# Merge with ten logit buffers, two output-weight buffers and an earlier split of the branch weights

## The chip, the core and the metric

The kernel runs on one core of one Trainium2 chip. Its engines work side by side, each through its own instructions in order: TensorE (PE) multiplies matrices, VectorE (DVE), ScalarE (ACT) and GpSimd (POOL) work on elements, and SyncE (SP) issues the transfers between the chip's main memory (HBM) and the core's memory (SBUF). The engines meet only at semaphores. TensorE writes its sums into PSUM, which has eight banks of 512 columns. The metric is the time of one launch in microseconds of the device, as the median of several runs.

## What is computed

Two layers of a network on 1024 latent rows and 256 context rows, each 1024 wide. Each layer normalises its rows, runs four branches (two kinds of attention, a gating MLP and a delta rule), and then merges them. The change is in the merge of each layer and in the memory around it:

```python
def merge(h, branches, pgate):
    silu_gates = jnp.split(jax.nn.silu(pgate), N_BRANCH, -1)
    acc = None
    for i in range(N_BRANCH):
        term = jax.nn.sigmoid(h @ w_gate[l, i]) * ((branches[i] * silu_gates[i]) @ w_branch[l, i])
        acc = term if acc is None else acc + term
    return acc @ w_out[l]

out_x = merge(hx, (ya_x, yb_x, yc_x, yd_x), px_g)
x_new = layer_norm(DEEPNORM_ALPHA * x + gt_x * out_x) * ln_g[l] + ln_b[l]
```

The last layer needs no context rows, so it merges 1024 rows where the first merges 1280.

## The kernel before

`build` runs the phases of a layer one after the other, with a barrier of all engines between them: `modulation`, `normalise_rows`, the four branches, `merge`, `output`. `normalise_rows` leaves the normalised rows, turned and split into a high and a low part, in `m.hh` and `m.hl` (40 KB of each partition for each). The class `Dense` spreads the products `h @ w_gate`, which are the logits of the merge gates, over the branches as filling work for TensorE and stores them in HBM as `gate_sums`. These products are all done when `apply_gates`, the first part of `merge`, ends. So the rows are no longer read in what follows.

The rest of `merge` is the place of the change. It goes through `products`, a list of triples (f, b, n): f is one of 8 blocks of 128 output columns, b one of 4 branches, n one of the chunks of rows (256, 512 and 512 rows in the first layer, two of 512 in the last). A block has 12 products in the first layer and 8 in the last, which makes 96 and 64 products, numbered u. For each product:

- SP loads the logits from `gate_sums` (line 2171) into one of `LOGITS = 4` buffers of 512 columns, once product u - 4 has been multiplied.
- ACT takes their sigmoid in place (line 2200).
- TensorE makes the branch product (lines 89 to 91: three matmuls for each of two row blocks of the weights, since an fp32 product is made of high and low parts), into bank u % 8.
- DVE multiplies the two (line 2241). For b = 0 the result goes to the block's accumulator `acc` (memory of `m.dv`), else to one of two term buffers (`TERMS = 2`, memory of `out_ds` and `raw_ds`), each of which must have been added before it is written again.
- POOL adds the term to the accumulator (line 2262).

Three more things run through the same queues. The weights of the four branches for a block (512 KB) are loaded by SP into one buffer `w` (line 2162) and split by `cut`: ACT writes the high part (line 2194), DVE the low part (line 2225), and TensorE begins a block only when its low part is there (`w_low`). The finished accumulator of block f - 1 is stored by SP at product b = 2, n = 0 of block f, after a wait for all its additions (line 2180). The weights of `output` are brought in 16 pieces of 256 KB, two for each block (`out_piece`: where u % EVERY is 3), through one buffer `wo` (line 2177), and split into the memory of `m.hh` and `m.hl` by ACT (line 2204) and DVE (line 2246). The order of all this is the order in which the loops are written. Before the change ACT splits the next block's weights after branch 2, and DVE after the first product of branch 3:

```python
if b == 2 and n == n_c - 1 and f + 1 < KD:    # scalar
    cut(f + 1)
if b == 3 and n == 0 and f + 1 < KD:          # vector
    cut(f + 1)
```

Of the kernel before, what the change touches and what calls it, by code (L numbers as in the profile page):

```python
# [5 lines left out]
F32 = mybir.dt.float32  # L6
F32R = mybir.dt.float32r
ALU = mybir.AluOpType
ACT = mybir.ActivationFunctionType
# [2106 lines left out]
                fill.cut(pool)  # L2116


def merge(nc, m, l):


    chunks = m.dense.chunks
# [2 lines left out]
    with ExitStack() as st:  # L2125
# [4 lines left out]
        halves = lambda x: x[:].rearrange("p (s a) b c -> p s (a b) c", s=2).rearrange("p s (b k) c -> p s b k c", k=2)  # L2130
        w = sb("w", [P, 4, 2, P])
        wh, wl = halves(m.dense.wh), halves(m.dense.wl)
        LOGITS, TERMS = 4, 2
        logit = sb("logit", [P, LOGITS, 512])
        term = [m.dense.out[:], m.dense.raw[:].rearrange("p k c -> p (k c)")]
        acc = m.dv[:].rearrange("p t c -> p (t c)").rearrange("p (s c) -> p s c", s=2)
        names = [f"logit_in{s}" for s in range(LOGITS)]
        wo = sb("wo", [P, 512])
        with phase(nc, "w_in", "w_high", "w_low", "sigm", "branched", "multiplied", "added", "stored0", "stored1",
                   "wo_in", "wo_high", "wo_low", *names) as (  # L2140
                block, w_in, w_high, w_low, sigm, branched, multiplied, added, stored0, stored1, wo_in, wo_high, wo_low,
                *logit_in):
            stored = [stored0, stored1]
            products = [(f, b, n) for f in range(KD) for b in range(4) for n in range(n_c)]
            EVERY = 2 * n_c

            def out_piece(u):

                i = u // EVERY
                return (i, i // 2, slice(i % 2 * 512, i % 2 * 512 + 512)) if u % EVERY == 3 else None  # L2150

            def nth(f, b, n):
                return (3 * f + b - 1) * n_c + n

            @block.sync
            def _(sp):
                sp.wait_ge(m.dense.stored, 16 * m.dense.units * n_c)

                def weights(f):
                    if f >= 1:  # L2160
                        sp.wait_ge(w_low, f)
                    sp.dma_start(w[:], m.d_wmerge[l, 4 * f:4 * f + 4, :, KD:KD + 2].rearrange("b p k c -> p b k c")
                                 ).then_inc(w_in, 16)

                weights(0)
                weights(1)
                for u, (f, b, n) in enumerate(products):
                    at, width = chunks[n]
                    if u >= LOGITS:
                        sp.wait_ge(multiplied, u - LOGITS + 1)  # L2170
                    sp.dma_start(logit[:, u % LOGITS, 0:width], m.d_raw[:, 8 + 4 * f + b, at:at + width]
                                 ).then_inc(logit_in[u % LOGITS], 16)
                    if out_piece(u):
                        i, k, part = out_piece(u)
                        if i:
                            sp.wait_ge(wo_low, i)
                        sp.dma_start(wo[:], m.d_wout[l, k, :, part]).then_inc(wo_in, 16)
                    if b == 2 and n == 0 and f >= 1:
                        sp.wait_ge(added, 3 * n_c * f)
                        sp.dma_start(m.d_acc[:, f - 1, lo:], acc[:, (f - 1) % 2, lo:]).then_inc(stored[(f - 1) % 2], 16)  # L2180
                        if f + 1 < KD:
                            weights(f + 1)
                sp.wait_ge(added, 3 * n_c * KD)
                sp.dma_start(m.d_acc[:, KD - 1, lo:], acc[:, (KD - 1) % 2, lo:]).then_inc(stored[(KD - 1) % 2], 16)
                for s in range(2):
                    sp.wait_ge(stored[s], 16 * KD // 2)

            @block.scalar
            def _(act):
                def cut(f):  # L2190
                    act.wait_ge(w_in, 16 * (f + 1))
                    if f >= 2:
                        act.wait_ge(branched, (f - 1) * 4 * n_c)
                    act.activation(wh[:, f % 2], w[:], ACT.Copy).then_inc(w_high, 1)

                cut(0)
                for u, (f, b, n) in enumerate(products):
                    act.wait_ge(logit_in[u % LOGITS], 16 * (u // LOGITS + 1))
                    own = logit[:, u % LOGITS, 0:chunks[n][1]]
                    act.activation(own, own, ACT.Sigmoid).then_inc(sigm, 1)  # L2200
                    if out_piece(u):
                        i, k, part = out_piece(u)
                        act.wait_ge(wo_in, 16 * (i + 1))
                        act.activation(m.hh[:, k, part], wo[:], ACT.Copy).then_inc(wo_high, 1)
                    if b == 2 and n == n_c - 1 and f + 1 < KD:
                        cut(f + 1)

            @block.tensor
            def _(pe):
                for u, (f, b, n) in enumerate(products):  # L2210
                    at, width = chunks[n]
                    if b == 0 and n == 0:
                        pe.wait_ge(w_low, f + 1)
                    if u >= 8:
                        pe.wait_ge(multiplied, u - 7)
                    for k in range(2):
                        mm = split_products(pe, m.ps[:, u % 8, 0:width], wh[:, f % 2, b, k], wl[:, f % 2, b, k],
                                            yh[:, 2 * b + k, at:at + width], yl[:, 2 * b + k, at:at + width], k == 0, k == 1)
                    mm.then_inc(branched, 1)

            @block.vector
            def _(dve):
                def cut(f):
                    dve.wait_ge(w_high, f + 1)
                    dve.tensor_tensor(wl[:, f % 2], w[:], wh[:, f % 2].bitcast(F32), ALU.subtract).then_inc(w_low, 1)  # L2225

                cut(0)
                for u, (f, b, n) in enumerate(products):
                    at, width = chunks[n]
                    dve.wait_ge(sigm, u + 1)  # L2230
                    dve.wait_ge(branched, u + 1)
                    if b == 0:
                        dst = acc[:, f % 2, at:at + width]
                        if f >= 2:
                            dve.wait_ge(stored[f % 2], 16 * (f // 2))
                    else:
                        at_term = nth(f, b, n)
                        dst = term[at_term % TERMS][:, 0:width]
                        if at_term >= TERMS:
                            dve.wait_ge(added, at_term - TERMS + 1)  # L2240
                    dve.tensor_tensor(dst, logit[:, u % LOGITS, 0:width], m.ps[:, u % 8, 0:width], ALU.mult
                                      ).then_inc(multiplied, 1)
                    if out_piece(u):
                        i, k, part = out_piece(u)
                        dve.wait_ge(wo_high, i + 1)
                        dve.tensor_tensor(m.hl[:, k, part], wo[:], m.hh[:, k, part].bitcast(F32), ALU.subtract
                                          ).then_inc(wo_low, 1)
                    if b == 3 and n == 0 and f + 1 < KD:
                        cut(f + 1)

            @block.gpsimd
            def _(pool):
                for u, (f, b, n) in enumerate(products):
                    at, width = chunks[n]
                    if b == 0:
                        continue
                    pool.wait_ge(multiplied, u + 1)
                    at_term = nth(f, b, n)
                    if b >= 2:
                        pool.wait_ge(added, at_term - n_c + 1)  # L2260
                    own = acc[:, f % 2, at:at + width]
                    pool.tensor_tensor(own, own, term[at_term % TERMS][:, 0:width], ALU.add).then_inc(added, 1)


def output(nc, m, l, out):

    tiles = range(0 if l < DEPTH - 1 else CT, NT)
    src = m.d_x if l == 0 else m.d_x1
    wo_h, wo_l = m.hh[:, :, 0:D], m.hl[:, :, 0:D]
    AHEAD = 4  # L2270
    with ExitStack() as st:
        sb = lambda n, s, d=F32: st.enter_context(nc.sbuf_tensor(f"{n}_ou{l}", s, d))
# [119 lines left out]
def build(nc, d_x, d_c, d_const, d_rope, d_vec, d_bvec, d_wmod, d_win, d_winr, d_ws, d_bs, d_wuq, d_wukv,  # L2392
# [12 lines left out]
    with ExitStack() as st:  # L2405
# [8 lines left out]
        m.gate_c = sb("gate_c", [P, 16])  # L2414
        m.dv = sb("dv", [P, NT, BR])
        m.ab = sb("ab", [P, NT, 16])
        m.hh = sb("hh", [P, KD, ROWS], F32R)
        m.hl = sb("hl", [P, KD, ROWS], F32R)
        with phase(nc, "loaded") as (block, loaded):
            @block.sync  # L2420
            def _(sp):
# [6 lines left out]
                dve.memset(m.eps[:], EPS)  # L2428
        for l in range(DEPTH):
            modulation(nc, m, l)  # L2430
            with ExitStack() as layer:
                m.dense = Dense(nc, m, l, layer)
                normalise_rows(nc, m, l)
                gating_mlp(nc, m, l)
                latent_attention(nc, m, l)
                differential_attention(nc, m, l)
                delta_net(nc, m, l)
                merge(nc, m, l)
                m.dense.free()
            output(nc, m, l, out)  # L2440
        return m


# [85 lines left out]
```

## Time and profile before

| | us |
|---|---|
| median of 3 runs | 4258.75 |
| lowest and highest | 4256.01, 4259.47 |
| profiled execution, its own time | 4253.75 |
| profiled execution, span in the trace | 4252.0 |

The span runs from the first to the last instruction; 1.75 us of the execution lie around it. The profile gives TensorE as busy for 82% of the span, VectorE 45%, ScalarE 26%, GpSimd 26%, and a mean granted TensorE clock of 0.907 of full speed. The two merges take from 1949 to 2122 us and from 4019 to 4144 us of the span. The profile is read from there: the busy time by stretches, who waited for whom, and the instructions in order of time.

### The profile page before, as it was taken

The page shows a single profiled execution, that of the slowest core. Times are in us where ns is not written, and L with a number is a line of the kernel's source. Part 1 is how long each engine was busy: PE and PEld are TensorE (multiplying, and loading weights), DVE is VectorE, ACT ScalarE, POOL GpSimd, SP SyncE. Part 2 cuts the span into 40 slices and gives each one's busy share as a digit, 9 for nine tenths or more (in the row PEclk, how much of TensorE's full clock was granted, in tenths as well). Part 3 has the DMA queues.
Part 4 walks back from the last instruction along what each step waited for, and adds up shares of the span by engine and source line. Part 5 has one row for each costly group of instructions (what it writes and reads, how often), then busy time and mean ns, then how long its engine had stood idle before and what let it go on. Part 6 is the DMA issues. An engine that isn't in the chain of part 4 may idle for free. (4 is left out here: it accounts for less than half of the span.)

```text
span 4252.0 us, 62711 instructions
## 1 busy us (share of the span) xinstructions
PE 3491.2 (82%) x25404; PEld 2722.3 (64%) x25404; DVE 1911.1 (45%) x3011; ACT 1120.4 (26%) x1986; POOL 1096.7 (26%) x1154
## 2 busy tenths in 40 slices
PE   5877889577869988998796788887778878889778
PEld 2775557366757777886672675566567657767666
DVE  3224442694365553113463323542881645542256
ACT  2202331472222212113311201321661321211241
POOL 1101101351134442233400202102440344433260
PEclk7978899699989999998897889998899989999999
DMA  4101002301021113335644101003101121114473
GB/s 178 46 33 41 7 17 73 79 27 58 25 64 54 57 48 97 120 116 158 201 153 168 62 30 49 6 26 104 46 26 47 54 73 52 64 41 136 134 237 139
DMA packets 205011, 334.39 MB, mean 79 GB/s; under 512 B 23360, under 2 KB 96832, under 8 KB 203072
## 3 DMA queue, kind: packets, MB, share of 16 engines
q1 hardware_dynamic: 175936, 283.34, 21.0%
q10 hardware_dynamic: 28800, 47.20, 3.0%
q8 instruction: 195, 3.19, 0.3%
q14 instruction: 80, 0.66, 0.0%
HBM read 249.45 MB, written 81.00 MB: 78 GB/s over the span
## 5 line engine op out<-in xcount | busy, mean ns | idle before, releaser
L89 PE MATMUL ps<-hh,wh_ds 128*128 128x512 f32 (+1 forms) x1600 | 666.4, 417 | 77.9 <-ACT out_ds L183 29.8
L90 PE MATMUL ps<-hl,wh_ds 128*128 128x512 f32 (+1 forms) x1600 | 606.3, 379 | 0.0
L91 PE MATMUL ps<-hh,wl_ds 128*128 128x512 f32 (+1 forms) x1600 | 604.8, 378 | 0.0
L89 PEld LDWEIGHTS ps<-hh,wh_ds 128*128 128x128 f32 x1600 | 313.0, 196 | 167.6 <-issue 50.2
L90 PEld LDWEIGHTS ps<-hl,wh_ds 128*128 128x128 f32 x1600 | 313.3, 196 | 59.3 <-issue 16.3
L91 PEld LDWEIGHTS ps<-hh,wl_ds 128*128 128x128 f32 x1600 | 311.7, 195 | 55.5
L196 POOL CAST wh_ds<-raw_ds 128x512 fp32r<-128x512 f32 x160 | 106.7, 667 | 757.1 <-PE ps L91 263.2
L183 ACT ACTIVATE out_ds<-ps 128x512 f32<-128x512 f32 (+1 forms) x200 | 110.3, 551 | 575.3 <-PE ps L91 519.9
L198 POOL TENSOR_TENSOR wl_ds<-raw_ds,wh_ds 128x512 fp32r<-128x512 f32 x160 | 210.4, 1315 | 12.8
L1035 DVE TENSOR_REDUCE nmx_d<-ps 128x1 f32<-128x1280 f32 (+1 forms) x144 | 193.9, 1366 | 40.2 <-PE ps L964 39.9
L2105 DVE TENSOR_TENSOR y_ag<-y_ag,gate_ag 128x512 f32<-128x512 f32 (+1 forms) x40 | 28.6, 715 | 406.6 <-ACT gate_ag L2087 406.6
L1103 ACT ACTIVATE qk_da<-ps,nmx_d 128x1280 f32<-128x1280 f32 (+1 forms) x144 | 177.4, 1232 | 74.0 <-DVE nmx_d L1035 73.6
L964 PE MATMUL ps<-k_la,qs_la 96*128 96x512 f32 (+1 forms) x400 | 173.9, 548 | 25.6 <-POOL qs_la L895 20.3
L89 PE MATMUL ps<-yh_mg,wh_ds 128*128 128x256 f32 (+1 forms) x320 | 132.8, 415 | 72.4 <-DVE wl_ds L2225 72.4
L964 PE MATMUL ps<-kk_da,qs_da 128*128 128x512 f32 (+1 forms) x400 | 122.3, 415 | 82.0 <-ACT qk_da L1103 50.1
L1969 DVE TENSOR_TENSOR T_dr<-T_dr,ps 128x256 f32<-128x256 f32 x200 | 84.0, 421 | 176.5 <-PE ps L1729 172.2
L1729 PE MATMUL ps<-V_dr,TC_dr 64*64 64x64 f32 x3200 | 117.3, 224 | 45.5 <-DVE V_dr L1963 45.5
L1729 PEld LDWEIGHTS ps<-V_dr,TC_dr 64*64 64x64 f32 x3200 | 103.4, 137 | 70.6 <-DVE V_dr L1963 56.6
L964 PEld LDWEIGHTS ps<-kk_da,qs_da 128*128 128x128 f32 x400 | 72.3, 208 | 111.7 <-POOL qs_da L904 42.1
L995 DVE COPY work_la<-ps 128x512 f32<-128x512 f32 (+1 forms) x136 | 91.7, 674 | 107.1 <-PE ps L929 106.9
L89 PE MATMUL ps<-hh,ah_ou 128*128 128x512 f32 x288 | 114.1, 396 | 28.4 <-DVE al_ou L2361 28.4
L1718 PEld LDWEIGHTS ps<-T_dr,A_dr 64*64 64x64 f32 x3200 | 105.8, 140 | 48.6 <-issue 29.6
(318 smaller groups left out, 7632.7 us busy)
## 6 DMA issues: line engine op xcount, KB each, us to landing
gate_sums<-out_ds ACTq DMA_DIRECT2D x160, 256.0 KB, 2.0
raw_ds<-in_d_wmerge SPq DMA_DIRECT2D x128, 256.0 KB, 2.7
logit_mg<-gate_sums SPq DMA_DIRECT2D x128, 256.0 KB, 3.5
w_mod<-in_d_wmod SPq DMA_DIRECT2D x12, 2048.0 KB, 20.2
R_dr<-decay_rows SPq DMA_DIRECT2D x80, 256.0 KB, 4.3
qk_da<-turned_qk SPq DMA_DIRECT2D x32, 320.0 KB, 7.2
q_raw_da<-turned_qk SPq DMA_DIRECT2D x288, 32.0 KB, 1.8
acc_ou<-merged SPq DMA_DIRECT2D x18, 512.0 KB, 4.7
```

Of the source, the lines that this page charges most:

```text
L89: pe.matmul(out, w_hi, x_hi, start=first, stop=False)
L90: pe.matmul(out, w_hi, x_lo, start=False, stop=False)
L91: return pe.matmul(out, w_lo, x_hi, start=False, stop=last)
L183: act.activation(self.out[:, 0:width], m.ps[:, self.bank(chunk), 0:width], ACT.Copy).then_inc(self.moved, 1)
L196: pool.tensor_copy(self.wh[:, s], self.raw[:]).then_inc(self.high, 1)
L198: pool.tensor_tensor(self.wl[:, s], self.raw[:], self.wh[:, s].bitcast(F32), ALU.subtract).then_inc(self.low, 1)
L964: mm = pe.matmul(scores(h, a)[:, at:at + width], qs[:, h] if maps == 1 else qs[:, u % 2, a], k_all(h, a)[:, at:at + width], start=True, st ...
L995: dve.tensor_copy(pt[:, h, at:at + count], turn_bank(g, count).rearrange("p (b c) -> p b c", b=count)).then_inc(moved_d, 1)
L1035: dve.reduce_max(nmx[:, h, a:a + 1], scores(h, a), AX.X, negate=True).then_inc(maximum, 1)
L1103: act.activation(e[:, h % 2, a], scores(h, a), ACT.Exp, bias=nmx[:, h, a:a + 1], accum_out=sums).then_inc(exp_done, 1)
L1718: mm = pe.matmul(level(d)[half(a), h * HD:(h + 1) * HD], A[d][half(a), h, half(a)], T[d][half(a), s % 2, h], start=True, stop=True)
L1729: mm = pe.matmul(level(d)[half(a), BR + h * HD:BR + (h + 1) * HD], TC[d][half(a), h], V[d][half(a), h], start=True, stop=True)
```

## The change

`merge` gets two stacks of buffers from `build`: `rows`, which holds `m.hh` and `m.hl`, now taken anew in each layer, and `weights`, which lives until `output` has ended. After `apply_gates` the rows are given back, and in their memory stand two tiles for the split output weights (32 KB of each partition for each) and, with what else is free, ten buffers of logits in place of four. `output` reads its weights from the new tiles. The output pieces are loaded into two buffers in turn, each with a semaphore of its own. The load of the next block's weights moves from b = 2 to b = 0 of each block, and the two splits move to the end of branch 1. Every instruction's size and the number of each kind stay as they were.

```diff
-        LOGITS, TERMS = 4, 2
+        LOGITS, TERMS = 10, 2
+        rows.close()
+        m.wo = [weights.enter_context(nc.sbuf_tensor(f"w_out_{n}{l}", [P, KD, D], F32R, side="right")) for n in ("high", "low")]
+        wo_h, wo_l = m.wo
-        wo = sb("wo", [P, 512])
+        wo = sb("wo", [P, 2, 512])
...
                 weights(0)
-                weights(1)
                 for u, (f, b, n) in enumerate(products):
...
-                        if i:
-                            sp.wait_ge(wo_low, i)
-                        sp.dma_start(wo[:], m.d_wout[l, k, :, part]).then_inc(wo_in, 16)
+                        if i >= 2:
+                            sp.wait_ge(wo_low, i - 1)
+                        sp.dma_start(wo[:, i % 2], m.d_wout[l, k, :, part]).then_inc(wo_in[i % 2], 16)
+                    if b == 0 and n == 0 and f + 1 < KD:
+                        weights(f + 1)
                     if b == 2 and n == 0 and f >= 1:
                         sp.wait_ge(added, 3 * n_c * f)
                         sp.dma_start(m.d_acc[:, f - 1, lo:], acc[:, (f - 1) % 2, lo:]).then_inc(stored[(f - 1) % 2], 16)
-                        if f + 1 < KD:
-                            weights(f + 1)
...
-                        act.activation(m.hh[:, k, part], wo[:], ACT.Copy).then_inc(wo_high, 1)
-                    if b == 2 and n == n_c - 1 and f + 1 < KD:
+                        act.activation(wo_h[:, k, part], wo[:, i % 2], ACT.Copy).then_inc(wo_high, 1)
+                    if b == 1 and n == n_c - 1 and f + 1 < KD:
                         cut(f + 1)
...
-                        dve.tensor_tensor(m.hl[:, k, part], wo[:], m.hh[:, k, part].bitcast(F32), ALU.subtract
+                        dve.tensor_tensor(wo_l[:, k, part], wo[:, i % 2], wo_h[:, k, part].bitcast(F32), ALU.subtract
                                           ).then_inc(wo_low, 1)
-                    if b == 3 and n == 0 and f + 1 < KD:
+                    if b == 1 and n == n_c - 1 and f + 1 < KD:
                         cut(f + 1)
```

What this moves is shown at two places of the first layer. On VectorE, from the first block's weights into the second block, before the change (`dv` is the accumulator, `out_ds` and `raw_ds` the two terms, `hl` the low part of the output weights):

```order
L2225 TENSOR_TENSOR wl_ds<-w_mg,wh_ds 128x1024
L2241 TENSOR_TENSOR dv<-logit_mg,ps 128x256
L2241 TENSOR_TENSOR dv<-logit_mg,ps 128x512 x2
L2241 TENSOR_TENSOR out_ds<-logit_mg,ps 128x256
L2246 TENSOR_TENSOR hl<-wo_mg,hh 128x512
L2241 TENSOR_TENSOR raw_ds<-logit_mg,ps 128x512
L2241 TENSOR_TENSOR out_ds<-logit_mg,ps 128x512
L2241 TENSOR_TENSOR raw_ds<-logit_mg,ps 128x256
L2241 TENSOR_TENSOR out_ds<-logit_mg,ps 128x512
L2241 TENSOR_TENSOR raw_ds<-logit_mg,ps 128x512
L2241 TENSOR_TENSOR out_ds<-logit_mg,ps 128x256
L2246 TENSOR_TENSOR hl<-wo_mg,hh 128x512
```

The second `L2225`, the split of the next block's weights, stands on the row behind these, with two products of the block left. After the change the same engine has there:

```order
L2227 TENSOR_TENSOR wl_ds<-w_mg,wh_ds 128x1024
L2243 TENSOR_TENSOR dv<-logit_mg,ps 128x256
L2243 TENSOR_TENSOR dv<-logit_mg,ps 128x512 x2
L2243 TENSOR_TENSOR out_ds<-logit_mg,ps 128x256
L2248 TENSOR_TENSOR w_out_low<-wo_mg,w_out_high 128x512
L2243 TENSOR_TENSOR raw_ds<-logit_mg,ps 128x512
L2243 TENSOR_TENSOR out_ds<-logit_mg,ps 128x512
L2227 TENSOR_TENSOR wl_ds<-w_mg,wh_ds 128x1024
```

The split of the next block's weights has moved ahead of the last six products of the block. On SP, from the second block's store to the output piece behind it, before the change:

```order
L2180 DMA merged<-dv 128x1280
L2162 DMA w_mg<-in_d_wmerge 128x4x256
L2171 DMA logit_mg<-gate_sums 128x512 x2
L2171 DMA logit_mg<-gate_sums 128x256
L2177 DMA wo_mg<-in_d_wout 128x512
```

After the change, from the second block's first logits:

```order
L2173 DMA logit_mg<-gate_sums 128x256
L2165 DMA w_mg<-in_d_wmerge 128x4x256
L2173 DMA logit_mg<-gate_sums 128x512 x2
L2173 DMA logit_mg<-gate_sums 128x256
L2179 DMA wo_mg<-in_d_wout 128x512
L2173 DMA logit_mg<-gate_sums 128x512 x2
L2173 DMA logit_mg<-gate_sums 128x256
L2184 DMA merged<-dv 128x1280
```

The load of the weights stands seven loads ahead of the store, where it stood right behind it.

## Rows read from the trace of the kernel before

**Rows 1.** Busy time by stretches, us; the first line names the columns

```profile
core 0: us, PE busy (x) PEld busy (x) DVE busy (x) ACT busy (x) POOL busy (x), PEclk, DMA share, GB/s
...
1956.00:2118.50 162.50, 133.84 (x576) 110.87 (x575) 81.56 (x119) 66.93 (x119) 84.69 (x72) 0.84 0.65 206
...
4026.00:4142.00 116.00, 96.26 (x384) 76.40 (x382) 65.27 (x87) 54.82 (x87) 74.26 (x48) 0.93 0.77 248
...
2028.00:2031.00 3.00, 3.00 (x18) 2.59 (x17) 0.49 (x1) 1.09 (x2) 0.52 (x1) 1.00 1.05 387
...
1955.60:1960.40 4.80, 4.79 (x14) 4.09 (x15) 0.14 (x1) 0.42 (x1) 0.00 (x0) 0.50 0.74 237
2015.70:2021.40 5.70, 5.70 (x17) 4.73 (x18) 2.23 (x4) 1.56 (x4) 2.52 (x2) 0.50 0.56 161
...
1880.00:1940.00 60.00, 60.00 (x311) 51.57 (x311) 6.41 (x10) 11.43 (x23) 14.44 (x14) 1.00 0.32 105
```

**Rows 2.** Waits in the first merge: who for whom, us, times, longest

```profile
ACT logit_mg L2200 <- DMA logit_mg<-gate_sums: 83.0, 51, 4.8
...
PE ps L89 <- DVE wl_ds L2225: 35.6, 8, 10.8
...
DVE raw_ds L2241 <- ACT logit_mg L2200: 15.1, 8, 4.2
```

**Rows 3.** Waits in the second merge

```profile
PE ps L89 <- DVE wl_ds L2225: 36.8, 8, 21.3
```

**Rows 4.** TensorE in order of time: start, us, instruction, idle before and its releaser

```profile
1955.61 0.58 PE L89 MATMUL ps<-yh_mg,wh_ds 128*128 128x256 f32 x1 [10.75 <-DVE wl_ds L2225]
1974.64 0.58 PE L89 MATMUL ps<-yh_mg,wh_ds 128*128 128x256 f32 x1 [2.74 <-DVE wl_ds L2225]
...
2022.05 0.28 PE L89 MATMUL ps<-yh_mg,wh_ds 128*128 128x256 f32 x1
...
2025.51 0.28 PE L89 MATMUL ps<-yh_mg,wh_ds 128*128 128x256 f32 x1
...
2114.28 0.39 PE L91 MATMUL ps<-yh_mg,wl_ds 128*128 128x512 f32 x1
...
4025.41 0.80 PE L89 MATMUL ps<-yh_mg,wh_ds 128*128 128x512 f32 x1 [21.34 <-DVE wl_ds L2225]
...
4028.93 0.39 PE L91 MATMUL ps<-yh_mg,wl_ds 128*128 128x512 f32 x1
4029.16 0.40 PE L89 MATMUL ps<-yh_mg,wh_ds 128*128 128x512 f32 x1
...
4031.89 0.39 PE L89 MATMUL ps<-yh_mg,wh_ds 128*128 128x512 f32 x1
...
4039.50 0.50 PE L89 MATMUL ps<-yh_mg,wh_ds 128*128 128x512 f32 x1 [1.33 <-DVE wl_ds L2225]
...
4137.36 0.39 PE L91 MATMUL ps<-yh_mg,wl_ds 128*128 128x512 f32 x1
```

**Rows 5.** Transfers in the first merge, 1956 to 2118 us: queue, packets, MB, share

```profile
q1 hardware_dynamic: 20832, 33.43, 65.2%
```

**Rows 6.** VectorE in order of time, first block of the second merge

```profile
4030.75 1.35 DVE L2241 TENSOR_TENSOR dv<-logit_mg,ps 128x512 f32<-128x512 f32 x2 [5.39 <-ACT logit_mg L2200]
...
4041.27 0.69 DVE L2241 TENSOR_TENSOR dv<-logit_mg,ps 128x512 f32<-128x512 f32 x1
```

**Rows 7.** By tile: durations ns min/median/max of the split and the additions

```profile
L2225 DVE TENSOR_TENSOR wl_ds<-w_mg,wh_ds x16: 1216/1378/1745, 1954.3 to 4125.3; 128x1024 fp32r<-128x1024 f32 x16
...
L2262 POOL TENSOR_TENSOR dv<-dv,out_ds x60: 734/1292/2266, 1964.5 to 4137.3; 128x512 f32<-128x512 f32 x48, 128x256 f32<-128x256 f32 x12
```

**Rows 8.** SP and ScalarE in order of time, around the store of a block

```profile
2043.83 0.43 SPq L2180 DMA_DIRECT2D merged<-dv  x1
...
2044.78 2.46 SPq L2171 DMA_DIRECT2D logit_mg<-gate_sums  x3
...
2050.58 1.35 ACT L2200 ACTIVATE logit_mg<-logit_mg 128x512 f32<-128x512 f32 x2 [4.61 <-DMA logit_mg<-gate_sums]
```

More of the change, by code:

```diff
@@ L2116, in _, with merge @@
                 fill.cut(pool)
-def merge(nc, m, l):
+def merge(nc, m, l, rows, weights):
     chunks = m.dense.chunks
@@ L2137, in merge @@
         names = [f"logit_in{s}" for s in range(LOGITS)]
-        wo = sb("wo", [P, 512])
+        wo = sb("wo", [P, 2, 512])
         with phase(nc, "w_in", "w_high", "w_low", "sigm", "branched", "multiplied", "added", "stored0", "stored1",
-                   "wo_in", "wo_high", "wo_low", *names) as (
-                block, w_in, w_high, w_low, sigm, branched, multiplied, added, stored0, stored1, wo_in, wo_high, wo_low,
+                   "wo_in0", "wo_in1", "wo_high", "wo_low", *names) as (
+                block, w_in, w_high, w_low, sigm, branched, multiplied, added, stored0, stored1, wo_in0, wo_in1, wo_high, wo_low,
                 *logit_in):
-            stored = [stored0, stored1]
+            stored, wo_in = [stored0, stored1], [wo_in0, wo_in1]
             products = [(f, b, n) for f in range(KD) for b in range(4) for n in range(n_c)]
@@ L2202, in _ @@
                         i, k, part = out_piece(u)
-                        act.wait_ge(wo_in, 16 * (i + 1))
-                        act.activation(m.hh[:, k, part], wo[:], ACT.Copy).then_inc(wo_high, 1)
-                    if b == 2 and n == n_c - 1 and f + 1 < KD:
+                        act.wait_ge(wo_in[i % 2], 16 * (i // 2 + 1))
+                        act.activation(wo_h[:, k, part], wo[:, i % 2], ACT.Copy).then_inc(wo_high, 1)
+                    if b == 1 and n == n_c - 1 and f + 1 < KD:
                         cut(f + 1)
@@ L2268, in output @@
     src = m.d_x if l == 0 else m.d_x1
-    wo_h, wo_l = m.hh[:, :, 0:D], m.hl[:, :, 0:D]
+    wo_h, wo_l = m.wo
     AHEAD = 4
@@ L2416, in build @@
         m.ab = sb("ab", [P, NT, 16])
-        m.hh = sb("hh", [P, KD, ROWS], F32R)
-        m.hl = sb("hl", [P, KD, ROWS], F32R)
         with phase(nc, "loaded") as (block, loaded):
@@ L2430, in build @@
             modulation(nc, m, l)
+            weights = st.enter_context(ExitStack())
             with ExitStack() as layer:
+                rows = layer.enter_context(ExitStack())
+                m.hh, m.hl = (rows.enter_context(nc.sbuf_tensor(f"{n}{l}", [P, KD, ROWS], F32R, side="right"))
+                              for n in ("hh", "hl"))
                 m.dense = Dense(nc, m, l, layer)
@@ L2437, in build @@
                 delta_net(nc, m, l)
-                merge(nc, m, l)
+                merge(nc, m, l, rows, weights)
                 m.dense.free()
             output(nc, m, l, out)
+            weights.close()
         return m
```

## The prediction

> **What bounds the kernel now.** I read the busy time by stretches first. In the stretch ahead of the first merge TensorE is busy for 60 of 60 us at the full clock of 2.4 GHz [rows 1], so nothing is lost there. In the merges it is busy for 134 of 162.5 us at a mean granted clock of 0.84, and for 96 of 116 us at 0.93 [rows 1]. The merges are therefore where TensorE loses both time and clock, and the change touches nothing else.
>
> Next the waits. TensorE waits eight times in each merge, always at the start of a block and always for the low part of that block's weights, which VectorE makes: 35.6 and 36.8 us [rows 2, 3]. The first wait of each is the start of the phase (10.8 and 21.3 us) and stays. The other seven add up to 24.8 and 15.5 us. The pauses also cost clock: after one of 2.74 us the matmuls restart slow [rows 4], and a block of the first merge runs its first 5.7 us at a clock of 0.50, which is 1.2 GHz [rows 1]. After a pause of 1.33 us they don't [rows 4].
>
> VectorE is late with the split because it stands behind ten products of the block, and each of those needs its sigmoid. ScalarE waits 83.0 us for logits in the first merge, and VectorE passes that on (15.1 us at one of its three destinations) [rows 2]. With four buffers a load is asked for only when the product four places back is done. So the chain is: logits late, VectorE late, split late, TensorE stopped, TensorE slow.
>
> **The floor without stops.** At the full clock one branch of the first merge takes 2025.51 - 2022.05 = 3.46 us, a block of four 13.84 us. In the second it is 4031.89 - 4029.16 = 2.73 us, a block 10.92 us [rows 4]. The first merge now takes TensorE from 1955.61 to 2114.67, 159.1 us. Eight blocks at full speed take 110.7, and the slow clock after the start stays: 4.8 us at half clock [rows 1], 2.4 us lost. That makes 113.1, 46.0 us less. The second now takes from 4025.41 to 4137.75, 112.3 us. Eight blocks take 87.4, and 3.5 us at half clock at the start (to 4028.93 [rows 4]) lose 1.8, so 89.2 and 23.1 us less. Both together are 69.1 us, the most that the change can bring, unless the end of the phase shrinks too.
>
> **Who could be late instead.** GpSimd adds for 84.69 / 8 = 10.6 us of each block in the first merge and 74.26 / 8 = 9.3 in the second; VectorE works for 10.2 and 8.2, ScalarE for 8.4 and 6.9 [rows 1]. All are under 13.84 and 10.92. With only two term buffers VectorE and GpSimd form a loop, and the loop counts, not the shares. Its length can be read once, in the first block of the second merge, where banks and logits were ready: from the first product at 4030.75 to the next block's first at 4041.27, 10.5 us [rows 6]. This is under 10.92, barely. For the first merge I walk it: 10.6 us of additions, in which GpSimd also runs dry for about 0.7 us behind each of two output pieces and 0.4 us at the block's three products without a term, 12.4 us in all, under 13.84.
>
> Transfers: 33.43 MB over eight blocks are 4.2 MB a block [rows 5]. The best 3 us of the merge moved 387 GB/s [rows 1], and 4.2 MB at that rate take 10.8 us. The second merge moved 248 GB/s for 116 us, 3.6 MB a block, 9.3 us. Now the queue runs at 65% and 77%; it would have to run at about 80% and 85%.
>
> **Part by part.** *Ten buffers*: no instruction more, 96 and 64 loads as before; they are worth the waits of ScalarE. But SP is in order, and two waits now stand in its way. The load of the next block's weights waits until VectorE has split the last ones, after branch 1 of the block before. SP gets there when VectorE is up to nine products behind it, so it is held until six (first merge) or four products are still ahead of VectorE. The wait for all additions of the last block, ahead of its store, is reached with six or four logits issued ahead. Queued behind it are the logits of the second half of the block. Before the change a store, a load of weights and then logits went out, the store at 2043.83 and the logits at 2044.78, and the sigmoid began at 2050.58 [rows 8]: 5.8 us from issue. The 1.2 MB ahead of it are 3.0 us of that at 387 GB/s, so with the store alone (0.66 MB) 4.5 us, in the second merge 4.2. VectorE wants that product at 6.3 us into the block of the second merge, and SP gets through its wait at 0.5 to 1.1 us, issues the logits 0.5 us later, has the sigmoid ready at 5.9 to 6.4. It is just in time. In the first merge the same walk leaves over 1 us.
>
> *The earlier split*: the same instructions, 1.2 to 1.7 us on VectorE [rows 7]. It now stands six (or four) products ahead of the block's end, at least 5.5 us of TensorE's work, where it had two. I cost the waits for it at nothing. Its cover is VectorE not falling behind by four products; if that goes, TensorE stops again at the block's start. ScalarE's half waits until TensorE has finished the block before, and queued behind it are sigmoids that lie up to ten products ahead, so nobody is held.
>
> *Two output buffers*: loads of pieces go out one piece earlier, and ScalarE's waits for them go under the same cover; nothing on the path. *Rows given back, memory elsewhere*: addresses only, and `output` reads the same amounts; nothing. *Seven more semaphores* to clear at the end of the phase: no row shows one alone. The 10.75 us in which TensorE stands still ahead of the merge [rows 4] hold the same clearing for the phase before, a barrier, a load and a split, so seven can be a small part only: I take 0 and leave 1 us for each merge. *The start*: the second load of weights was already issued before logits and still is, and one logit load comes earlier, which no one on the path waits for; 0 to -1 us. *The tail* from TensorE's last product to the last addition (now some 3.5 us) is set by GpSimd's last terms and stays, within 1 us both ways.
>
> **The sum.** Floor -69.1. For small stops I leave 0.15 us a block in the first merge, where margins are 1.4 us, and 0.35 in the second, where loop and logits are both just in time: 1.2 + 2.8 = 4.0 us. This gives -65. The profiled execution took 4253.75, so 4188.75; the median of the runs lies 5.0 higher, so 4193.75, say 4194 us.
>
> **Rivals.** *A, the two terms set the pace.* The loop measured at 10.5 us had one addition after the other without a gap. If the split in mid-block and the output piece right ahead of it (both after product 3 in the second merge, some 3 us of VectorE while only two terms wait) let GpSimd run dry, a block is 9.3 us of additions, 1.4 of products without a term and 1.3 dry: 12.0 us. Eight of them and 1.8 make 97.8, which saves 14.5 there; with 44.8 in the first merge, -59 and 4200. For it: an addition takes 1.29 us alone and up to 2.27 beside VectorE's subtractions [rows 7]. The Trainium skill (SBUF — State Buffer, "Who interferes with whom") says that a VectorE instruction with two inputs in SBUF and a GpSimd instruction that reads SBUF exclude each other for a whole instruction; the trace agrees, 2.27 being about 1.29 and a subtraction. Against it: rows 6 contain both kinds.
>
> *B, ten buffers in name only.* SP's two waits keep logits late once a block. Then a stop remains in each block, half as long as now, and the clock falls after it in the first merge: 7 x (1.8 + 3.0) + 7 x 1.1 = 41 us of the 69 stay, -28, 4231. For it: the 0 to 0.5 us of slack worked out above. Against it: only one product is that tight and eight banks lie between.
>
> *C, slower: the clock.* If TensorE is paced by VectorE it makes short pauses at the banks all the time, and its clock could stay at 1.2 GHz. Matmuls then take twice as long: 8 x (13.84 + 10.92) x 2 = 396 us in place of 271, +125, 4384. It decides when more than about 138 us of the merges run at the half clock, since each costs half a microsecond and the gain is 69. Against it: the pauses of 1.33 us that didn't lower the clock [rows 4]. The Trainium skill (TensorE: Matmul & The Clock Gate, "A second HAM failure mode: psum-queue depth-cycling") describes a kernel whose frequent short pauses between groups made the clock swing; by that rule case A would turn into this one. No row here shows it.
>
> **Chances.** Forecast 0.73, A 0.15, B 0.09, C 0.03. The low end is the floor with the spread of the runs, 4184; the range reaches over A to 4214 and leaves B and C out. About 0.2% (8.5 us) is what a measurement of this kernel can tell from no change. Faster by more holds in the first three, nearly: 0.95; within it 0.02; slower 0.03.
>
> **What would show it.** Right: TensorE's waits for the low part of the weights fall to the first of each merge; the granted clock of both merges is above 0.95; TensorE's stretches are 113 to 115 and 90 to 93 us; ScalarE still waits for logits, but VectorE for ScalarE hardly. A shows as products of VectorE waiting for GpSimd in the second merge, B as TensorE stopped at banks while VectorE waits for sigmoids in mid-block, C as a clock near 0.5. I am wrong if transfers can't hold 320 GB/s with a store among them: then VectorE waits for logits all along.

## The result

The changed kernel takes 4194.44 us (median of 4 runs, 4191.38 to 4197.83), the kernel before in the same comparison 4257.38 (4 runs, 4246.59 to 4259.47). The ratio is 0.9857 with a 95% interval of 0.9839 to 0.9876: faster by 1.4%. The forecast was 4194 with a range of 4184 to 4214. That the median falls within half a microsecond of the forecast is partly luck: single runs differ by 6 us and more, two terms of the sum were off against each other, and the forecast put the median 5.0 us above the profiled execution, where it lies 3.1 above (4191.38).

First TensorE's stops. These are all its rows with a wait before them within the two merges of the changed kernel, in order of time, and the last row of each merge (columns as in [rows 4]; in the second merge the line of the low part is now L2227):

```profile
1953.93 0.58 PE L89 MATMUL ps<-yh_mg,wh_ds 128*128 128x256 f32 x1 [10.79 <-DVE wl_ds L2227]
...
2066.63 0.39 PE L91 MATMUL ps<-yh_mg,wl_ds 128*128 128x512 f32 x1
...
3978.65 0.80 PE L89 MATMUL ps<-yh_mg,wh_ds 128*128 128x512 f32 x1 [21.41 <-DVE wl_ds L2227]
...
4037.37 0.50 PE L89 MATMUL ps<-yh_mg,wh_ds 128*128 128x512 f32 x1 [1.78 <-DVE wl_ds L2227]
4061.12 0.50 PE L89 MATMUL ps<-yh_mg,wh_ds 128*128 128x512 f32 x1 [1.56 <-DVE wl_ds L2227]
...
4071.93 0.39 PE L91 MATMUL ps<-yh_mg,wl_ds 128*128 128x512 f32 x1
```

In the first merge only the start is left of eight waits [rows 2, 4]; in the second two of 1.8 and 1.6 us remain besides the start. TensorE now takes from 1953.93 to 2067.02, 113.1 us, where the floor worked out ahead was 113.1; and from 3978.65 to 4072.32, 93.7 us, where the floor was 89.2. A second trace of the same kernel has 112.4 and 92.0. The clock and the transfers came along, in the busy time by stretches (columns as in [rows 1]):

```profile
1953.90:2067.00 113.10, 113.07 (x576) 96.63 (x576) 78.08 (x118) 66.73 (x120) 89.09 (x71) 0.98 0.87 296
3978.60:4072.30 93.70, 90.31 (x384) 72.96 (x384) 70.71 (x84) 54.34 (x85) 63.77 (x45) 0.98 0.88 298
```

TensorE is busy for 113.07 of 113.10 us in the first merge. The clock is 0.98 in both, where it was 0.84 and 0.93, and the transfers run at 296 and 298 GB/s, where they ran at 206 and 248 [rows 1]. In the first merge ScalarE's wait for logits fell from 83.0 us [rows 2] to 36.3:

```profile
ACT logit_mg L2202 <- DMA logit_mg<-gate_sums: 36.3, 19, 4.1
...
DVE raw_ds L2243 <- ACT logit_mg L2202: 1.8, 2, 1.0
```

A wait of ScalarE costs nothing as long as it is far enough ahead. The last row shows that: VectorE's wait for sigmoids at this destination was 15.1 us [rows 2] and is 1.8. Over all three destinations it fell from 44.3 us to 8.6, and in the second merge from 25.1 to 9.2.

For the kernels below I cut each trace at four places in SP's order: the first load of branch weights in each merge, and the first load of `merged` in each `output`. So a merge holds its start and its tail too. All numbers are us of the traces:

| kernel | to merge 1 | merge 1 | between | merge 2 | output 2 | span |
|---|---|---|---|---|---|---|
| before | 1949.3 | 173.2 | 1896.7 | 125.1 | 107.7 | 4252.0 |
| changed | 1947.6 | 126.2 | 1898.5 | 108.7 | 108.6 | 4189.6 |
| changed, second trace | 1942.0 | 125.5 | 1897.4 | 107.1 | 109.3 | 4181.4 |
| four logit buffers | 1949.7 | 145.5 | 1898.3 | 116.4 | 108.6 | 4218.5 |
| late load and split | 1952.7 | 140.1 | 1903.6 | 116.5 | 108.4 | 4221.3 |
| six logit buffers | 1954.2 | 126.6 | 1896.6 | 108.2 | 109.1 | 4194.7 |
| three terms | 1950.6 | 125.6 | 1898.8 | 107.4 | 108.8 | 4191.2 |
| pieces moved | 1951.7 | 126.4 | 1899.5 | 105.3 | 108.0 | 4190.9 |
| two weight buffers | 1954.2 | 125.9 | 1894.9 | 105.3 | 108.3 | 4188.5 |
| pieces, three terms | 1951.6 | 126.7 | 1901.4 | 105.9 | 108.8 | 4194.4 |
| all three | 1953.4 | 125.5 | 1900.8 | 103.5 | 109.7 | 4192.9 |
| all three, second trace | 1961.4 | 125.4 | 1895.2 | 103.4 | 109.1 | 4194.6 |
| one term | 1947.3 | 168.7 | 1901.7 | 134.8 | 108.6 | 4261.1 |

The table shows where the time went: 47.0 us from the first merge and 16.4 from the second (18.0 in the second trace). It also shows how far the parts that no edit touches wander: 1942.0 to 1961.4 us up to the first merge. The merges of one kernel repeat within 0.1 to 1.6 us. So small effects are read in the merges and not in the medians.

### The profile page after: what moved, and what is told of

It reads as the page before. It is cut to its first block and busy times, and to the rows that moved or that the text cites. A ratio compares the mean times of both kernels' runs of the same rounds, so it can differ in the third digit from the quotient of the medians.

```text
span 4189.6 us, 62711 instructions
## 1 busy us (share of the span) xinstructions
PE 3465.9 (83%) x25404; PEld 2699.9 (64%) x25404; DVE 1916.8 (46%) x3011; ACT 1122.5 (27%) x1986; POOL 1103.6 (26%) x1154
## 5 line engine op out<-in xcount | busy, mean ns | idle before, releaser
L196 POOL CAST wh_ds<-raw_ds 128x512 fp32r<-128x512 f32 x160 | 108.2, 676 | 761.7 <-PE ps L91 262.1
L964 PE MATMUL ps<-k_la,qs_la 96*128 96x512 f32 (+1 forms) x400 | 174.3, 549 | 24.8 <-POOL qs_la L895 20.3
L89 PE MATMUL ps<-yh_mg,wh_ds 128*128 128x256 f32 (+1 forms) x320 | 120.5, 377 | 35.5 <-DVE wl_ds L2227 35.5
L89 PE MATMUL ps<-w_out_high,ah_ou 128*128 128x512 f32 x288 | 114.3, 397 | 29.8 <-DVE al_ou L2363 29.8
```

Source lines behind the costliest of these rows:

```text
L89: pe.matmul(out, w_hi, x_hi, start=first, stop=False)
L196: pool.tensor_copy(self.wh[:, s], self.raw[:]).then_inc(self.high, 1)
L964: mm = pe.matmul(scores(h, a)[:, at:at + width], qs[:, h] if maps == 1 else qs[:, u % 2, a], k_all(h, a)[:, at:at + width], start=True, st ...
```

## The experiments

**One half each.** The first question is which part earned it. Four buffers of logits, all else as changed:

```diff
-        LOGITS, TERMS = 10, 2
+        LOGITS, TERMS = 4, 2
```

> The changed kernel with four buffers of logits in place of ten; the earlier load and split and the two output buffers stay. Theory (the late split stops TensorE, and ten buffers are what keeps the products behind it supplied): the waits for the low part of the weights at the starts of blocks shrink, but the supply of logits sets the pace and most of the 64 us don't come: 4215 to 4250 us. Rival (the place of the split alone is worth it, B read the other way round): 4200 us or less.

And ten buffers, with the load of the weights and the splits at their old places:

```diff
                 weights(0)
+                weights(1)
...
-                    if b == 0 and n == 0 and f + 1 < KD:
-                        weights(f + 1)
                     if b == 2 and n == 0 and f >= 1:
...
+                        if f + 1 < KD:
+                            weights(f + 1)
...
-                    if b == 1 and n == n_c - 1 and f + 1 < KD:    # scalar
+                    if b == 2 and n == n_c - 1 and f + 1 < KD:
...
-                    if b == 1 and n == n_c - 1 and f + 1 < KD:    # vector
+                    if b == 3 and n == 0 and f + 1 < KD:
```

> The changed kernel with the load of the weights and both splits at their places of before (branch 2 and the first product of branch 3); ten buffers of logits stay. Theory: VectorE is no longer held up by logits, but the split still stands two products before the block's end, so TensorE stops at each block's start, for less than now; a half to three quarters of the gain comes: 4205 to 4225 us. Rival (logits alone are the cause, the split's place is nothing once they are early): 4194 us, as the changed kernel.

They took 4222.55 us (ratio 0.992, 0.9893 to 0.9947) and 4223.57 us (0.9926, 0.9903 to 0.9949), beside 4256.30 for the kernel before: each half brings a little over half of the 63 us, neither brings them alone. By the table the first merge falls by 27.7 and 33.1 us, the second by 8.7 and 8.6, together 36.4 and 41.7. Their sum, 78, is more than the 63.4 of both at once. The overlap is in the first merge (60.8 against 47.0), where either edit shortens the same stops; in the second the two nearly add up (17.3 against 16.4, or 18.0 in the second trace). Both kernels keep the two output-weight buffers, and no run takes these away alone. With four logit buffers they can't free SP earlier in the first merge: SP asks for a piece only after the product four places back, and the last piece's subtraction stands ahead of that product in VectorE's order. So they aren't counted twice there; what they add beside ten buffers isn't shown. With ten buffers and the late split TensorE still waits at every block of the first merge. Of the two fences below, the first is that wait with the late split, the second the same wait with four buffers and the early split, where six of eight remain (us in total, times, longest), both for the first merge:

```profile
PE ps L89 <- DVE wl_ds L2228: 21.5, 8, 10.7
```

```profile
PE ps L89 <- DVE wl_ds L2227: 21.5, 6, 10.9
```

Both totals hold the start, 10.7 and 10.9. What is left, some 10.7 us, was 24.8 before and is zero with both edits. With four buffers TensorE's stretch of the first merge is 127.8 us, 14.7 more than in the changed kernel: 10.6 of them are these stops, and the rest is time in which it is busy, partly at the half clock. GpSimd then ends 6.9 us behind TensorE, where it was 2.4. Ahead of both stands VectorE, which waits for sigmoids for 18.1 us at the accumulator's products alone, where the changed kernel had 5.3:

```profile
DVE dv L2243 <- ACT logit_mg L2202: 18.1, 12, 3.1
```

Both theories' ranges hold the measured times, and both rivals (either half is everything) fall. One expectation was off in size: with four buffers a little over half of the gain came, where I had written that most of it wouldn't.

**How many buffers are buffers.** Six in place of ten:

```diff
-        LOGITS, TERMS = 10, 2
+        LOGITS, TERMS = 6, 2
```

> The changed kernel with six buffers of logits. SP is held by its own two waits when six (first merge) or four to five (second) products are left, so if ten buffers are ten in name only (case B), six give nearly all of it: 4194 to 4200 us. If every buffer counts, it lies a third of the way from four buffers (4222) to ten: 4210 us.

The median is 4201.03 us (ratio 0.9881, 0.9861 to 0.99), 1 us above the range for "nearly all" and 9 below the 4210 of "every buffer counts". It is also 6.6 us above the changed kernel's, in a comparison in which the kernel before took 4252.94 and not 4257.38. In its one trace the merges, 126.6 and 108.2 us, are those of ten buffers (125.5 to 126.2 and 107.1 to 108.7), and 6.6 us more lie ahead of the first merge. The intervals of the ratios overlap. I count the difference as wander, which the trace supports and the medians don't exclude.

I had expected that SP's own waits hold the queue at about six loads ahead. By SP's and VectorE's rows that is so in the second merge of the changed kernel, where at most 12 of 64 loads are issued while seven or more logits, this one counted, aren't multiplied yet. In the first it isn't: there at least 60 of 96 are, and up to ten are ahead. So rival B was right in number for the second merge alone. In the first, buffers seven to ten are used and still bring nothing in the merge's time.

**One term buffer: does a paced TensorE lose its clock?** This is the mechanism by which the change could have been slower.

```diff
-        LOGITS, TERMS = 10, 2
+        LOGITS, TERMS = 10, 1
```

> The changed kernel with one term buffer: VectorE can't write a term before the last one has been added, so the loop of VectorE and GpSimd takes about 2.1 us for each 512-column term, some 20 us a block in the first merge, and TensorE must stop at its banks after each product. Case C (frequent short pauses bring the clock down): the granted clock of the merges falls to 0.5 to 0.7. Against it: the clock stays above 0.9 though TensorE is idle for a quarter of the time; the time is 4240 to 4260 us by the loop alone.

It took 4262.89 us in its one run, 3 us above the range that the loop alone was to give; TensorE was idle for 16% of its stretch of the first merge, where I had expected a quarter. In the first merge TensorE now stops at its banks, with some 25 waits for VectorE's products of up to 1.2 us, and yet keeps its clock. These are stretches of that kernel, the whole first merge, the second, and 20 us within the first:

```profile
1953.60:2099.00 145.40, 121.89 (x576) 95.96 (x576) 68.77 (x112) 63.96 (x116) 84.19 (x66) 0.98 0.67 225
4024.10:4138.60 114.50, 97.98 (x384) 77.86 (x384) 63.93 (x82) 53.75 (x84) 61.67 (x44) 0.91 0.71 241
1980.00:2000.00 20.00, 16.29 (x78) 12.62 (x77) 10.29 (x18) 8.49 (x15) 12.07 (x11) 1.00 0.63 217
```

```profile
PE ps L89 <- DVE out_ds L2243: 18.7, 25, 1.2
```

For 20 us it is busy for 16.3 and the granted clock is 1.00. In the second merge TensorE stops at six block starts, for 0.9 to 3.6 us, and there the clock is 0.91. Case C falls for pauses of up to 1.2 us. The Trainium skill (TensorE: Matmul & The Clock Gate, "A second HAM failure mode: psum-queue depth-cycling") describes a kernel in which frequent short pauses between groups of matmuls made the clock swing. In this trace they don't. The run also shows what the term buffers are worth: with one, the first merge takes 168.7 us in place of 126.2.

**What holds the second merge 4.5 us above its floor.** VectorE's rows of one block of it in the changed kernel (columns: start, us, engine, line, out and in):

```profile
4031.82 0.69 DVE L2243 TENSOR_TENSOR dv<-logit_mg,ps 128x512 f32<-128x512 f32 x1 [1.82 <-ACT logit_mg L2202]
...
4033.78 1.32 DVE L2248 TENSOR_TENSOR w_out_low<-wo_mg,w_out_high 128x512 fp32r<-128x512 f32 x1
4035.03 2.29 DVE L2227 TENSOR_TENSOR wl_ds<-w_mg,wh_ds 128x1024 fp32r<-128x1024 f32 x1
```

And GpSimd's at the same place:

```profile
4034.51 1.73 POOL L2264 TENSOR_TENSOR dv<-dv,raw_ds 128x512 f32<-128x512 f32 x1
4038.00 1.30 POOL L2264 TENSOR_TENSOR dv<-dv,out_ds 128x512 f32<-128x512 f32 x1 [1.76 <-DVE out_ds L2243]
```

Both causes that the prediction priced stand here side by side. The product at 4031.82 came 1.82 us late because its sigmoid was late (B). Its logits had been asked for late: SP was held until the split before had ended, at 4024.37, and then issued the weights and the logits behind them:

```profile
4024.39 0.38 SPq L2165 DMA_DIRECT2D w_mg<-in_d_wmerge  x1
4024.82 2.26 SPq L2173 DMA_DIRECT2D logit_mg<-gate_sums  x3
```

The piece and the split then stand one behind the other for 3.5 us, the split lasts 2.29 us where its median was 1.38 [rows 7], and GpSimd runs dry for 1.76 us (A). The two are tied: a longer split also holds SP longer. Three edits tell them apart. A third term:

```diff
-        LOGITS, TERMS = 10, 2
+        LOGITS, TERMS = 10, 3
...
-        term = [m.dense.out[:], m.dense.raw[:].rearrange("p k c -> p (k c)")]
+        more = sb("more", [P, TERMS - 2, 512])
+        term = [m.dense.out[:], m.dense.raw[:].rearrange("p k c -> p (k c)")] + [more[:, i] for i in range(TERMS - 2)]
```

> The changed kernel with a third term buffer between VectorE and GpSimd. In the second merge VectorE's loop with GpSimd takes 11.0 us a block where TensorE needs 10.9, and GpSimd stands idle 1.76 us of each block behind the output piece and the split. If the two terms set the pace there (case A), the merge loses up to 8 x 0.5 = 4 us: 4190 us, and GpSimd's gaps shrink. If held logits (case B) make the rest, no change: 4194 us within 1.5.

The output pieces two products earlier:

```diff
-                return (i, i // 2, slice(i % 2 * 512, i % 2 * 512 + 512)) if u % EVERY == 3 else None
+                return (i, i // 2, slice(i % 2 * 512, i % 2 * 512 + 512)) if u % EVERY == 1 else None
```

> The changed kernel with the output pieces at the places where u modulo EVERY is 1 in place of 3: in the second merge VectorE's subtraction of a piece no longer stands right ahead of the split, but at the products of branch 0 and 2. Case A by way of GpSimd running dry for 1.76 us a block: that gap goes to below 0.5 us, 4188 to 4191 us. If the gap costs nothing because the loop is held elsewhere, by logits or by TensorE: 4194 us within 1.5.

Two buffers for the branch weights, so that SP isn't held until the last split is done (nine logit buffers, to make room):

```diff
-        w = sb("w", [P, 4, 2, P])
+        w = sb("w", [P, 2, 4, 2, P])
-        LOGITS, TERMS = 10, 2
+        LOGITS, TERMS = 9, 2
...
-                    if f >= 1:
-                        sp.wait_ge(w_low, f)
-                    sp.dma_start(w[:], m.d_wmerge[l, 4 * f:4 * f + 4, :, KD:KD + 2].rearrange("b p k c -> p b k c")
-                                 ).then_inc(w_in, 16)
+                    if f >= 2:
+                        sp.wait_ge(w_low, f - 1)
+                    sp.dma_start(w[:, f % 2], m.d_wmerge[l, 4 * f:4 * f + 4, :, KD:KD + 2].rearrange("b p k c -> p b k c")
+                                 ).then_inc(w_in[f % 2], 16)
...
```

> The changed kernel with two buffers of branch weights and nine logit buffers, pieces and terms as in the changed kernel. By the trace: if SP's hold on the weights' load (B) is what makes VectorE wait for sigmoids at the second product of some blocks of the second merge, these waits (6.3 us for the accumulator's products) fall below 2 us, and TensorE's stretch of 93.7 us falls by 1 to 2. If the loop of VectorE and GpSimd (A) makes the 4.5 us above the floor, the stretch stays within 0.5 us.

The medians can't tell these apart: 4193.05 us (4186.53 to 4203.82) for three terms, 4199.57 (4192.73 to 4205.97) for the pieces, and 4190.27 in one run for the weights. The 4188 to 4191 us expected of the moved pieces didn't come. The traces can, in part, with one trace of each. TensorE's stretches of the second merge are 92.2, 89.6 and 90.3 us, against 93.7 and 92.0 in the two traces of the changed kernel:

```profile
3981.40:4073.70 92.30, 89.89 (x384) 72.67 (x384) 71.06 (x84) 54.75 (x86) 63.92 (x45) 0.98 0.89 303
```

```profile
3984.00:4073.50 89.50, 89.33 (x384) 72.75 (x384) 63.17 (x83) 53.60 (x84) 66.60 (x45) 0.98 0.92 310
```

```profile
3981.20:4071.50 90.30, 89.76 (x384) 72.99 (x384) 70.93 (x84) 54.09 (x85) 63.90 (x45) 0.98 0.88 299
```

The fences are the three kernels in that order. The third term brings nothing beyond what two executions of one kernel differ by; GpSimd is still dry behind piece and split. Moving the pieces brings TensorE to its floor and VectorE from 70.7 to 63.2 us of work for the same instructions, since its subtractions and GpSimd's additions now meet otherwise: the split takes 1.5 us in place of 2.3, and GpSimd is busy for 66.6 us in place of 63.8.

```profile
4049.41 1.52 DVE L2227 TENSOR_TENSOR wl_ds<-w_mg,wh_ds 128x1024 fp32r<-128x1024 f32 x1 [0.26 <-ACT wh_ds L2196]
```

GpSimd's gap behind the split is gone too. VectorE still waits for sigmoids, 7.8 us at the accumulator's products, so these waits alone don't stop TensorE. It is the place of the piece right ahead of the split that costs, not the number of terms. The second weight buffer brings TensorE to 90.3, and VectorE's waits for sigmoids at the accumulator's products fall to 0.6 us, where the changed kernel has 6.3 (4.7 in its second trace):

```profile
DVE dv L2243 <- ACT logit_mg L2202: 0.6, 2, 0.4
```

The moved pieces are worth 2.4 to 4.1 us of TensorE's stretch, and three more traces with moved pieces, below, have 89.0 to 89.9 us. The second weight buffer is worth 1.7 to 3.4 us, in one trace, where two executions of the changed kernel differ by 1.6; its mechanism is plain in the waits, its size isn't settled. Together they bring no more of TensorE's stretch than the pieces alone, so the two overlap.

**Together.** The pieces with three terms, then with two weight buffers and eight logit buffers as well:

> The changed kernel with the output pieces at u modulo EVERY = 1 and a third term buffer, ten logit buffers. In the trace of the pieces alone TensorE's stretch of the second merge was 89.6 us (the floor is 89.2) but GpSimd ended 5.3 us behind it, where it was 4.7 in the changed kernel and 2.5 before. If the two terms cause that lag, it falls to about 3 us; the second merge, to the end of additions, takes 92.5 us in place of 98.3, 4189 us. If GpSimd's own work is the bound there (9.3 us of additions a block), the lag stays above 5 us and the sum is 94.9, as with the pieces alone.

> As the run before this one (pieces moved, three terms), with two buffers for the branch weights, so that SP isn't held until the last split is done, and eight logit buffers to make room. If SP's hold still costs (case B; VectorE waited for logits 1.5 to 1.8 us at the second product of some blocks), the waits of VectorE for sigmoids in the second merge fall from 12 us to below 6, and the merge ends 1 to 2 us earlier than with ten logits and one buffer. If not: the same to 0.5 us.

> Pieces moved, three terms, two buffers of branch weights, eight logit buffers, once more. In its first trace the second merge took 93.0 us to the last addition where the changed kernel took 98.3, but the rest of the kernel wandered by more than that between executions. If the 5 us are real, its median lies 3 to 7 us (0.1%) under the changed kernel's of the same call; if something takes them back, they are equal within 1 us.

> The changed kernel once more, beside the next kernel on the same chip. Its ratio to the kernel before: 0.985 to 0.988. Its second merge, from TensorE's first matmul to the last addition, again about 98 us.

Pieces and three terms took 4196.25 us (4189.94 to 4201.56) with a second merge of 105.9 us, so the third term again brings nothing (105.3 without it). GpSimd's lag behind TensorE at the end stayed at 5.7 us (5.3 with the pieces alone, 4.7 in the changed kernel, 2.5 before). By what I had written ahead, its own additions would then be the bound there. The trace speaks against it. In the last block VectorE waits 2.73 us for a sigmoid, and GpSimd then stands idle for 0.82 and, behind a piece, 1.22 us between its last four additions:

```profile
4075.74 0.69 DVE L2244 TENSOR_TENSOR out_ds<-logit_mg,ps 128x512 f32<-128x512 f32 x1 [2.73 <-ACT logit_mg L2203]
```

With the second weight buffer as well the lag is 3.5 and 4.0 us. VectorE's waits for sigmoids in the second merge, expected to fall below 6 us, fell from 17.2 to 13.7 only (11.5 in the second trace). All three edits took 4195.56 us and, beside the changed kernel on one chip, 4194.87 (4192.03 to 4196.54) against 4192.22 (4183.21 to 4202.77). In the second merge they are worth 3.6 to 5.3 us, 103.4 and 103.5 against 107.1 and 108.7, and TensorE reaches its floor:

```profile
3988.40:4077.40 89.00, 89.00 (x384) 73.25 (x384) 64.19 (x85) 54.76 (x85) 67.35 (x46) 0.98 0.89 307
```

Expected were 3 to 7 us in the median; measured were 2.7 us the other way, and both are less than the runs scatter. In the two traces the kernel with all three reached the first merge 19.4 us later (1961.4 against 1942.0), in code that is the same in both, with a granted clock of 0.914 against 0.916 for the span. Of the 19.4 us, 11.1 are TensorE's busy time for the same 12428 matmuls (1621.2 against 1610.1). The two traces of the kernel with all three differ there by 8.0 us among themselves, so much of it is chance from execution to execution; whether the places of the tiles have a part isn't settled, since no run changed them alone. I can't show a version that beats the changed kernel.

## Why the prediction was right, point by point

- **What bounds the kernel.** The chain (logits late, VectorE late, split late, TensorE stopped, TensorE slow) is shown by the two halves: cutting it at the logits or at the split's place takes away a bit more than half, and the clock rises to 0.96 or 0.97 in either.
- **The floor.** 113.1 us for the first merge was met in one trace, and the other traces without a stop there have 112.4 to 113.7. In the second 89.2 was right as a floor (89.0 to 89.9 in four traces of other versions) and not reached by the changed kernel, whose 93.7 us lie above the 90 to 93 given as a sign of being right (92.0 in the second trace lie within).
- **Small stops.** In the first merge I left 1.2 us and there were none. In the second I left 2.8 and there were 4.5 in one trace and 2.8 in the other. What I took as just in time was just late: the waits of up to 1.8 us for sigmoids, and the loop of VectorE and GpSimd, where I used 10.5 us from a block whose order changes. A piece and the next split had stood three products apart there; the change put them back to back, and I had priced that in case A only.
- **The tail** was mis-sized. I wrote that it stays within 1 us. It fell by 1.1 us in the first merge and grew by 2.1 in the second, to 4.65 us. I had GpSimd's last terms as what sets it. In the second merge it was the last block's logits as well: their loads stand behind the store, which waited for the additions until 4067.29, so ScalarE stood idle for 4.51 us before their first sigmoid and VectorE for 1.62 (0.79 before the change), with TensorE's last matmul already over at 4072.32 and three of its products not yet multiplied.

```profile
4071.37 0.63 ACT L2202 ACTIVATE logit_mg<-logit_mg 128x512 f32<-128x512 f32 x1 [4.51 <-DMA logit_mg<-gate_sums]
...
4072.04 0.69 DVE L2243 TENSOR_TENSOR raw_ds<-logit_mg,ps 128x512 f32<-128x512 f32 x1 [1.62 <-ACT logit_mg L2202]
```

  This is read from rows; no run moved the store alone. Counted to the last addition, the second merge gained 16.5 us and not 20.3, the first 47.0 and not 44.8. The sum, 63.5, is close to the 65.1 forecast since the two errors, 2.2 and 3.8 us, partly cancel.
- **Transfers.** The queue was to run at about 80% and 85%; it ran at 87% and 88%, at 296 and 298 GB/s. VectorE didn't wait for logits all along, which was the sign named for transfers that can't keep up.
- **What costs nothing.** The rows' memory, seven semaphores, the start: between the merges and after them the changed kernel takes 1.8 and 0.9 us more in the trace. The other versions, with the same phases, show 1894.9 to 1903.6 and 108.0 to 109.7, so nothing is shown beyond wander, though `output` was never as short as the 107.7 us of the one trace of before.
- **The rivals.** A happened in the second merge, by the piece that stands back to back with the split and not by the number of terms; it was priced at 8.6 us there, and moving the pieces gave 2.4 to 4.1 us of TensorE's stretch. B named a limit that holds in the second merge and a small loss there, not the stop in each block that it was priced at. C didn't come, and the one-term kernel shows that it doesn't at pauses of up to 1.2 us either.

## What to carry to other kernels

When a step that the next block needs stands late in an engine's order, look at what that engine waits for ahead of it: moving the step and supplying the wait's cause each bring part, and their gains can overlap. Ask of a deeper queue how deep it must be: here six buffers gave the merge times of ten, even where up to ten were in use. And once the stops are gone, what still comes late in the last block shows in the tail.

## What the runs showed of the hardware

TensorE kept a granted clock of 1.00 over 20 us in which it was busy for 81% of the time, with pauses of up to about 1.2 us; in the first merge of the kernel before it fell to 0.50 at the block starts after pauses of 2.74 to 4.14 us. For shorter pauses the length alone doesn't tell. In the 3.4 us from the restart the granted clock was 0.52 after a pause of 2.01 us (six logit buffers, second merge), but 1.00 after one of 2.06 us (late load and split, first merge) and after one of 2.88 us (before, second merge).

The same split of 128 x 1024 elements on VectorE takes 1.22 us alone, and also where an addition of GpSimd starts 0.16 us after it, which then takes 2.2 us in place of 1.3. It takes 1.5 us where an addition that already runs ends some 0.45 us into it, and 2.3 us where that addition ends 1.2 us into it. By these rows the one that started first keeps its time and the other is lengthened. In one merge VectorE's busy time fell by 7.5 of 70.7 us with the same instructions in another order, while GpSimd's rose by 2.8.
